# RWKV stage of a two-layer float32 network: the values from unsplit weights, one transposition for the blocks to invert, shared decay factors, low-rank products in pairs, another order of TensorE's work

## What is computed

```python
r, k, v = jnp.einsum('sbtc,scd->sbtd', h[None] + dx[None] * mu[:3, None, None, :], w_rkv)
xw, xa, xg = h + dx * mu[3], h + dx * mu[4], h + dx * mu[5]
w_log = -jax.nn.softplus(-(w0 + jnp.tanh(xw @ w1) @ w2)) - 0.5
decay = jnp.exp(-jnp.exp(w_log))
a = jax.nn.sigmoid(a0 + (xa @ a1) @ a2)
g = jax.nn.sigmoid(xg @ g1) @ g2
kk = normalised per head (k * k_k);  k = k * (1 + (a - 1) * k_a)
y = wkv7_scan(heads(r), heads(decay), heads(k), heads(v), -kk, kk * a_h)
# per head, per token: S = S diag(decay) + (S a) b^T + v k^T ;  y = S r
y = head_norm(y) * ln_g + ln_b + bonus(r, k, r_k) * v
return (y * g) @ w_o
```

## Time and profile before

| | |
|---|---|
| median of 3 runs | 2293.16 us (2292.47 to 2293.2) |
| the profiled execution's own time | 2288.61 us, of which its span is 2287.3 us |
| TensorE busy in the span | 2161.5 us (94%) |
| VectorE, ScalarE, GpSimd busy | 1576.3, 1119.0, 354.0 us |
| the RWKV stage in the span | about 205 us (end of the feed-forward layer before it) to 491 us (last matmul of `w_o`) |

### The profile page before, as it was taken

One profiled execution on the slowest core, in us unless ns is written; L12 is line 12 of the kernel. 1 busy time (PEld: TensorE's weight loads), 2 busy tenths in 40 slices (PEclk: granted clock), 3 DMA queues, 4 the chain that ended last, 5 costly groups with the idle time before them and its releaser, 6 DMA issues.

```text
span 2287.3 us, 33768 instructions
## 1 busy us (share of the span) xinstructions
PE 2161.5 (94%) x13268; PEld 1888.5 (83%) x13268; DVE 1576.3 (69%) x2595; ACT 1119.0 (49%) x1767; POOL 354.0 (15%) x166
## 2 busy tenths in 40 slices
PE   8997988899999999789999878899999999999999
PEld 6886768888888888568888667898999999888887
DVE  5667784466676766767666685589998996555554
ACT  5554542145554555546555684444444444444443
POOL 0000102200001000100003111223222222222222
PEclk9998996799999999879999998999999999999999
DMA  5665131036655666315665323444444444555554
GB/s 196 190 188 176 65 113 54 1 120 192 186 165 167 195 191 192 109 56 179 189 191 197 120 83 111 158 162 167 161 157 143 144 139 172 193 195 193 193 194 157
DMA packets 96652, 352.04 MB, mean 154 GB/s; under 512 B 10880, under 2 KB 11776, under 8 KB 96048
## 3 DMA queue, kind: packets, MB, share of 16 engines
q1 hardware_dynamic: 96496, 349.90, 46.7%
HBM read 348.81 MB, written 1.05 MB: 153 GB/s over the span
## 4 chain that ended last, share of the span: by engine, by line
PE 81%; DVE 13%; ACT 4%; issue 1%; POOL 1%; DMA 0%; SPq 0%; ACTq 0%; DVEq 0%
PE psum L235 17%; PE psum L237 16%; PE psum L236 16%; PE psum L279 14%; PE psum L278 6%; DVE tile_low L185 3%; PE psum L2517 2%; PE psum L995 2%; ACT tile_high L173 1%; PE psum L282 1%; POOL small L1596 1%; PE psum L321 1%; PE psum L759 1%; PE psum L1756 1%; PE psum L1740 1%
## 5 line engine op out<-in xcount | busy, mean ns | idle before, releaser
L185 DVE TENSOR_TENSOR tile_low<-raw_tiles,tile_high 128x1024 fp32r<-128x1024 f32 x543 | 677.0, 1249 | 370.5 <-ACT tile_high L173 364.0
L173 ACT ACTIVATE tile_high<-raw_tiles 128x1024 fp32r<-128x1024 f32 x650 | 686.3, 1056 | 465.4 <-PE psum L237 464.9
L279 PE MATMUL psum<-hT,tile_high 128*128 128x512 f32 x1408 | 494.0, 395 | 5.9 <-DVE tile_low L185 5.9
L197 POOL TENSOR_TENSOR tile_low<-raw_tiles,tile_high 128x1024 fp32r<-128x1024 f32 x107 | 270.9, 2531 | 761.1 <-ACT tile_high L173 761.1
L235 PE MATMUL psum<-hT,tile_high 128*128 128x256 f32 x1280 | 373.4, 292 | 8.5 <-DVE tile_low L185 3.9
L236 PE MATMUL psum<-hT,tile_high 128*128 128x256 f32 x1280 | 366.0, 286 | 0.0
L237 PE MATMUL psum<-hT,tile_low 128*128 128x256 f32 x1280 | 365.6, 286 | 0.0
L235 PE MATMUL psum<-tile_high,hT 128*128 128x512 f32 (+1 forms) x848 | 336.9, 397 | 17.8 <-DVE mix_arena L2333 9.3
L278 PE MATMUL psum<-hT,tile_low 128*128 128x256 f32 x1232 | 343.9, 279 | 0.0
L237 PE MATMUL psum<-tile_high,hT 128*128 128x512 f32 (+1 forms) x848 | 333.1, 393 | 0.0
L236 PE MATMUL psum<-tile_low,hT 128*128 128x512 f32 (+1 forms) x848 | 332.9, 393 | 0.0
(11 more groups left out here) (335 smaller groups left out, 2631.7 us busy)
## 6 DMA issues: line engine op xcount, KB each, us to landing
raw_tiles<-ffn_in_dram SPq DMA_DIRECT2D x176, 512.0 KB, 3.6
raw_tiles<-peer_u_dram SPq DMA_DIRECT2D x128, 512.0 KB, 3.2
raw_tiles<-peer_v_dram SPq DMA_DIRECT2D x128, 512.0 KB, 3.7
raw_tiles<-ffn_out_dram SPq DMA_DIRECT2D x88, 512.0 KB, 3.5
raw_tiles<-w_kv_dram SPq DMA_DIRECT2D x16, 512.0 KB, 3.3
raw_tiles<-in_gates_dram SPq DMA_DIRECT2D x16, 512.0 KB, 3.2
raw_tiles<-peer_q_dram SPq DMA_DIRECT2D x16, 512.0 KB, 3.2
raw_tiles<-w_k_dram SPq DMA_DIRECT2D x8, 512.0 KB, 4.1
```

The costliest lines, as they stand in the source:

```text
L173: scalar.activation(k.high[:, n % SLOTS, :], k.raw[:, n % RAW_SLOTS, :], ACT.Copy).then_inc(*k.tile_high_made.mark(n))
L185: vector.tensor_tensor(k.low[:, n % SLOTS, :], k.raw[:, n % RAW_SLOTS, :], k.high[:, n % SLOTS, :].bitcast(F32), ALU.subtract).then_inc(*k ...
L197: pool.tensor_tensor(k.low[:, n % SLOTS, :], k.raw[:, n % RAW_SLOTS, :], k.high[:, n % SLOTS, :].bitcast(F32), ALU.subtract).then_inc(*k.p ...
L279: ins = k.tensor.matmul(ps, high[:, c, :], both[:, c, :, :], start=(c == 0), stop=(c == KC - 1), skip_group_check=True)
```

## The change

1. **`w_v` unsplit.** For the eight tiles of `w_v` neither `tile_high` nor `tile_low` is made (`unsplit`, `take_whole`), nor the two parts of the mixed activation: TensorE multiplies the raw tile with the whole activation in plain float32. The first product of a bank is one matmul of 512 columns, each other one two of 256. A slot of `raw_tiles` is then free only once TensorE has used the tile.
2. **One transposition.** ScalarE copies the diagonal blocks of `MT` together (`diagonal`, 4 copies), and VectorE turns them in one instruction.
3. **Decays shared.** The decay up to the token before (`before`, `p_before`: a VectorE subtraction and a ScalarE exponential of 128 x 2048 each) is read from the column before in `p_in`, and the first token's from 16 extra values (`first`). The mask `keep` comes from memory eight times repeated instead of being copied 15 times by VectorE, and the prefix sum is two instructions.
4. **Low-rank products in pairs.** `lora_w` and `lora_a` alternate, one on output partitions 0 to 63 and one on 64 to 127, and in the second product one on rows 0 to 63 and one on 64 to 127.
5. **`r` out of PSUM by VectorE.** `scale_r` multiplies each pair of `w_r` chunks from PSUM with the rated key (for the bonus) and with `p_in`; ScalarE's copies, GpSimd's product `rk` (L1535) and one VectorE product over 128 x 2048 go.
6. **Order.** `MAK` of block 0 is made ahead of `w_v`; after `w_v` come the bonus, the transpositions of `b` and `k`, `w`, `MRK`, then the inverses. At the end both halves of `y` of block 0 are turned after `y` of block 1. The masking, the substitution and ScalarE's program follow. The load of `ln` waits for the bonus, not for the last tile of `w_v`.

The diff, cut to its core:

```diff
+def unsplit(n):
+
+    return FIRST["w_v"][0] <= n < FIRST["w_v"][1]
...
     if n >= RAW_SLOTS:
-        sync.wait_ge(*low_made(k, n - RAW_SLOTS))
+        last = n - RAW_SLOTS
+        sync.wait_ge(*(k.tile_used.at(last) if unsplit(last) else low_made(k, last)))
...
+def take_whole(k):
+
+    n = k.taken
+    k.taken += 1
+    k.tensor.wait_ge(*k.landed[n % RAW_SLOTS].at(n))
+    return n, k.raw[:, n % RAW_SLOTS, :]
...
-    low_rank("lora_w", 3, lambda c: r["w_in"][:, c, 0:64], 64)
-    low_rank("lora_a", 4, lambda c: r["w_in"][:, c, 64:P], 64)
+    pair = (("lora_w", 3, slice(0, 64)), ("lora_a", 4, slice(64, P)))
+    ps = [bank(k, name, k.lora_hidden, name) for name, _, _ in pair]
...
+    for c in range(KC):
+        for i, (name, n, rows) in enumerate(pair):
+            ins = tensor.matmul(ps[i][rows, 0:T], r["w_in"][:, c, rows], r["whole"][MIXED[n]][:, c, :], start=(c == 0),
+                                stop=(c == KC - 1))
...
+    tensor.wait_ge(*k.scaled.at("k"))
+    tensor_scan_products(k, 0, "MAK", "k_s", "a_s", k.masked)
+    values = r["whole"][MIXED[2]]
     for g in range(2):
         ps = [bank(k, ("w_v", tb, g), k.v_out, ("w_v", tb, g)) for tb in range(TB)]
         for c0 in range(0, KC, 2):
-            n, pair = take(k)
-            pair = tuple(t.rearrange("p (k n) -> p k n", k=2) for t in pair)
...
+            n, tile = take_whole(k)
+            tile = tile.rearrange("p (k n) -> p k n", k=2)
...
+                    still, last = values[:, c0 + c, block(tb)], c0 + c == KC - 1
+                    if c0 + c == 0:
+                        tensor.matmul(ps[tb], still, tile[:, c, :], start=True, stop=False, skip_group_check=True)
+                    else:
+                        for cols in (slice(0, T), slice(T, 2 * T)):
+                            ins = tensor.matmul(ps[tb][:, cols], still, tile[:, c, cols], start=False, stop=last,
+                                                skip_group_check=True)
...
-    tensor.wait_ge(*k.scaled.at("k"))
-    tensor_scan_products(k, 0, "MAK", "k_s", "a_s", k.masked)
-    tensor.wait_ge(*k.scaled.at("r"))
+    tensor_bonus_and_tokens(k)
+    w(0)
     tensor_scan_products(k, 0, "MRK", "k_s", "r_s", k.masked)
-    w(0)
-    tensor_bonus_and_tokens(k)
...
-    tensor_turn_y(k, 0, 0)
     y(1)
-    tensor_turn_y(k, 0, 1)
+    for half in range(2):
+        tensor_turn_y(k, 0, half)
...
+    def scale_r(g):
+        vector.wait_ge(*k.tile_used.at(first_r + 2 * g + 1))
+        cols, ps = half_of(g), result(k, ("w_r", g))
+        vector.tensor_tensor(r["rk_flat"][:, cols], ps, r["k_rated"][:, cols], ALU.mult).then_inc(*k.rk_made.mark("rk"))
+        vector.tensor_tensor(r["u"](2)[:, cols], ps, r["p_in"][:, cols], ALU.mult).then_inc(*k.scaled.mark(("r", g)))
```

More of the change, by code:

```diff
@@ L182, in split_low @@
         n = k.low_at
-        if not on_pool(n):
+        if not on_pool(n) and not unsplit(n):
             vector.wait_ge(*k.tile_high_made.at(n))
@@ L762, in tensor_rwkv @@
     tensor.wait_ge(*k.loaded["w_in"].at("w_in"))
-    low_rank("lora_w", 3, lambda c: r["w_in"][:, c, 0:64], 64)
-    low_rank("lora_a", 4, lambda c: r["w_in"][:, c, 64:P], 64)
+    pair = (("lora_w", 3, slice(0, 64)), ("lora_a", 4, slice(64, P)))
+    ps = [bank(k, name, k.lora_hidden, name) for name, _, _ in pair]
+    for name, n, _ in pair:
+        tensor.wait_ge(*k.mixed.at((n, 1)))
+    for c in range(KC):
+        for i, (name, n, rows) in enumerate(pair):
+            ins = tensor.matmul(ps[i][rows, 0:T], r["w_in"][:, c, rows], r["whole"][MIXED[n]][:, c, :], start=(c == 0),
+                                stop=(c == KC - 1))
+    ins.then_inc(*k.lora_done.mark("lora_w", "lora_a"))
     tensor.wait_ge(*k.loaded["lo"].at("lo"))
-    for name, what, at in (("lora_w", r["hidden_w"], 0), ("lora_a", r["hidden_a"], D)):
+    for name, _, _ in pair:
         tensor.wait_ge(*k.lora_hidden.at(name))
[L768 to L773, removed]
+    for c in range(0, KC, 2):
+        ps = [bank(k, (name, c), k.lora_out, (name, c)) for name, _, _ in pair]
+        for i in range(2):
+            for j, (_, _, rows) in enumerate(pair):
+                ins = tensor.matmul(ps[j][:, i * T:(i + 1) * T], r["w_lo"][rows, (c + i) * P:(c + i + 1) * P],
+                                    r[("hidden_w", "hidden_a")[j]], start=True, stop=True)
+        ins.then_inc(*k.lora_used.mark(("lora_w", c), ("lora_a", c)))
     ps = bank(k, "norms", k.key_norm, "largest")
@@ L804, in tensor_rwkv @@
     for g in range(4):
-        ps = bank(k, ("w_r", g), k.features_out, ("w_r", g))
+        ps = bank(k, ("w_r", g), k.scaled, ("r", g))
         feature_major(k, ps[:, 0:T], k.hT, mix_ready(0) if g == 0 else None)
@@ L1062, in vector_rwkv @@
     h, dx = r["h"], r["dx"]
-    first_k, first_r, first_v = (FIRST[name][0] for name in ("w_k", "w_r", "w_v"))
+    first_k, first_r = (FIRST[name][0] for name in ("w_k", "w_r"))
     vector_norm(k, "rwkv", r["xn"], h, col(k, "mix_norm", 0), first_k + SLOTS, parts=False)
@@ L1249, in vector_scan @@
         pass
+    for half in range(2):
+        vector_head_var(k, 1, half)
+    for half in range(2):
+        vector_y_low(k, 0, half)
     for _ in zip(vector_last_norm(k, 0), vector_last_norm(k, 1)):
@@ L1441, in scalar_rwkv @@
                               ACT.Copy).then_inc(*k.mt_made.mark(("MT", tb, g)))
-    evac_r(2)
-    evac_r(3)
+    scalar.wait_ge(*k.mt_made.now())
+    for quarter in range(QUARTERS):
+        if quarter == 2:
+            split_high(k, first_r + 5 + SLOTS)
+        rows = rows_of(quarter)
+        ins = scalar.activation(r["diagonal"][rows, :, :], r["MT"][rows, :, rows], ACT.Copy)
+    ins.then_inc(*k.mt_made.mark("diagonal"))
     for g in range(2):
-        last = first_v + 4 * g + 3
-        split_high(k, last + SLOTS)
-        scalar.wait_ge(*k.tile_used.at(last))
+        scalar.wait_ge(*k.tile_used.at(first_v + 4 * g + 3))
         for tb in range(TB):
@@ L1498, in scalar_scan @@
                 *k.tokens_out.mark((name, i)))
+    for half in range(2):
+        per_head("w", 0, half, r["wbuf"])
     take_out_inverses(k, 0, copy, small_inverses)
```

139 lines of the change are left out of this document (54 added, 85 removed).

## The result

The changed kernel takes 2262.43 us (median of 4 runs, 2259.61 to 2264.48), the kernel before 2292.93 (4 runs beside it). The ratio is 0.9861, with a 95% interval of 0.9848 to 0.9875: 1.4% faster; the medians differ by 30.5 us. The forecast was 2264, with a range of 2251 to 2277. The profiled execution took 2260.79 us with a span of 2259.5, against 2288.61 and 2287.3: 27.8 us less.

What follows compares the result with a forecast made beforehand. TensorE, busy 94% of the span, bounds the kernel, with waits and half-clock stretches, and VectorE holds the w_v stretch. Gains of 19.9, 6.3 and 5.4, less 2.5, make 29.1 us: 2264 forecast, range 2251 to 2277.

Steps and rivals of the forecast that it cites:

- Low-rank pairs: lora_w and lora_a: two stretches of 7.05 and 7.10 us become 3.55 each; lora_g leads by 4.6, limited by ScalarE.
- `w_r` and `MAK`: End of w_r: a lead of 6.0 us, chosen between 3 and 8; then MAK takes about 1.9.
- `w_v`: Unsplit w_v: 29.6 us at TensorE's own pace, ending at 337.0, a gain of 19.9 us up to there.
- VectorE hidden: VectorE's substitution, done at about 334, is asked for by the inverses at 347.6: some 13 us of cover.
- Bonus to `MRK`: Bonus, transpositions, w(0) and MRK after w_v: 10.6 us at full clock, 6.3 more gained.
- The 2.5 us set aside for dips: Taken off the gain for a clock dip in the 16-column bonus and one more like it.
- Inverses to `u(1)`: From the inverses to the end of u(1): same work and waits, 64.2 us, costed at nothing.
- The end: End of the scan: y(1) 19.3 us, its clock falling soon after the start, then 9.9; a gain of 5.4.
- the other case: y(1) at full clock: 10.9 us instead of 20.37 at half, a gain of 13.8 at the scan's end.
- The sum: Whole kernel: 19.9 + 6.3 + 5.4 = 31.6, less 2.5 for the clock, a gain of 29.1 us.
- The likeliest case: Whole kernel: the forecast itself, 2264 us, spanning 2259 to 2269; chance 0.52.
- the first rival: The clock holds through y(1), with no idle ahead of it: 8.4 us more gained, 2253; chance 0.14.

Runs made afterwards that it cites:

- e5: Changed kernel with the first products of lora_w and lora_a one after the other instead of alternating: ratio 0.9857, 2260.1 us.
- e4: Changed kernel with every product of w_v as one matmul of 512 columns instead of two of 256: ratio 0.9849, 2258.3 us.
- e7: Changed kernel with the transposition of the diagonal blocks repeated 5 times more on VectorE, each behind the last: ratio 0.9854, 2259.5 us.
- e8: Changed kernel with the transposition of the diagonal blocks repeated 10 times more on VectorE, each behind the last: ratio 0.9907, 2271.6 us.
- e6: Changed kernel with the second products of lora_w and lora_a one after the other instead of alternating: ratio 0.9867, 2262.4 us.
- e11: e3 with block 0's two y turns between the parts of y(1), and VectorE and ScalarE taking block 0's y first: ratio 0.9818, 2251.2 us.
- e3: Changed kernel with the 64 records of y(1) that don't read u(1) issued ahead of the wait for it: ratio 0.9809, 2249.1 us.
- e1: Kernel before with w_v unsplit and nothing else of the change, except rk moved to another buffer: ratio 0.9946, 2280.5 us.
- e2: Changed kernel with the old end of the scan, y of block 0 turned ahead of y(1): ratio 0.9893, 2268.4 us.

## Why the prediction was right

The terms are taken in the prediction's own order, from the profiled execution. The stage began 1.5 us later than before, 242.29 against 240.83, so leads are counted from there where it matters.

- **Low-rank pairs.** `lora_g` 17.7 us after the stage's first product before, 13.6 after: a lead of 4.1, forecast 4.6. ScalarE as the limit is right for the changed kernel, which idles 1.23 us there; before, TensorE came to `lora_g` without a wait. That the columns overlap, `e5` shows.
- **`w_r` and `MAK`.** `MAK` at 306.81, a lead of 6.2 counted so, forecast 6.0. The value between 3 and 8 was chosen, so this is luck in part.
- **`w_v`.** 27.7 us against 29.6: this term was mis-sized. Records of 256 columns cost 11.22/52 = 0.216 here, not 0.226, and of 512 columns 0.43, not 0.527 (`e4`). It ends at 336.5, forecast 337.0, because the later start makes up for the shorter length.
- **VectorE hidden.** Ready at 334.7, forecast 334. The cover of 13 us ahead of the inverses was right (12.7), and 10 us are hidden (`e7`). But beyond the cover the first to wait is `w_v`, at about 15 us, for the bank of the last quarter of `r`, and not the inverses (`e8`).
- **Bonus to `MRK`.** 10.9 us, forecast 10.6 at full clock. The 2.5 us set aside for dips weren't needed in this execution. The same steps took 12.5 us in the traces of `e5`, `e6`, `e7` and `e11`, and 16.5 in `e3`'s (336.38 to 352.89), so an allowance is right; its size was a guess. `e1` shows that this gain needs more than the unsplit tiles: with them alone the steps stay at half clock, since a wait of 4.9 us stands before them.
- **Inverses to `u(1)`.** 64.7 us, forecast 64.2.
- **The end.** `y(1)` 20.7 at half clock, forecast 19.3; then 10.5, forecast 9.9. `e2` confirms what the move is worth (5.2 of wait). The prediction had the clock fall soon after the start. That is what `e4` to `e8` show (18.7 to 18.9 us); in the changed kernel's trace it is down from the first record. The reason that the prediction gave was thin, and it named the other case as open; `e3` shows that the clock holds when the pause is filled and the records are reordered.
- **The sum.** 29.2 us at the second half of `w_o`, forecast 29.1, and 27.8 in the span. That the sum is so near is luck in part. Counted from the stage's own start the lead is 30.6: `w_v` and the unused allowance gave some 4 us more than forecast, the inverses and the end took some 2.6 back, and the late start hides the rest. Behind the stage the two traces drift, with a lead of 31.6 at a later layer's first transposition (1184.35 against 1215.98); what causes that was not traced.

The likeliest case came true; the first rival (full clock through `y(1)`) was one small reordering away.

## What to carry to other kernels

When an engine's work is taken off the path, ask at which clock the engine that now leads will go on: here the 6 us gained at full clock behind `w_v` did not come with the unsplit tiles alone, because a wait still stood between. A pause of under a microsecond ahead of a long run of short matmuls can go with a loss of eight to ten; where work that doesn't depend on the awaited result can fill it, that is cheap to try. And before raising a clock, divide each step's duration by its records at both clocks: some don't gain from it.

## What was not expected of the hardware

- Matmuls of 32x32 took 0.055 us a record at 2.4 GHz and 0.056 at 1.2 GHz; those of 64x64 0.067 (16 in 1.07) and 0.118 (16 in 1.89).
- A 512-column plain float32 record cost 0.432 us in a run of its kind (`e4`) and 0.53 in the gate's products, where weights of 128 and of 32 rows alternate.
- Two matmuls with all 128 rows and different column halves overlapped: 3.67 us alternating, 6.3 one after the other.
- With a pause of 0.9 us ahead of `y(1)` its clock was 0.50, from the first record or after 1 to 2 us, in seven traces; without it, and with the records reordered, 1.00 in four. Pauses of 0.78 and 1.23 us elsewhere left it at 1.00.
- A VectorE instruction over 128x8 took 0.17 us, and 2.27 beside a GpSimd instruction over 128x1024, ending with it (`e3`).
